# A transformer block on one core: the adaLN front in four channel quarters, head 0 accumulated in six banks

## The chip, the cores and the metric

The program runs on one core of a Trainium2 chip. The core has five engines that run their own instruction streams and meet only through semaphores: TensorE (PE, matmuls), VectorE (DVE), ScalarE (ACT), GpSimd (POOL) and SyncE (SP), which here only issues DMAs. The metric is the device time of one execution in microseconds; lower is better. In the rows, PEld is TensorE's weight load, and SPq is SyncE's queue of DMA issues.

## The reference, cut to what matters

One block (depth 1) on 512 tokens of width 2048, all in float32. Every matrix product that matters is done as three float32r products of a high and a low part.

```
mod = silu(c) @ w_ada + b_ada                    # w_ada (2048, 12288)
sh1, sc1, gt1, sh2, sc2, gt2 = split(mod, 6)     # 2048 channels each
h = rmsnorm(x, g_norm1) * (1 + sc1) + sh1
proj = h @ w_in                                  # mq, mk, mv, mo, 16 gates, aq, ak, av
q, k = silu(conv5(mq)), silu(conv5(mk)) / 16     # 4 heads of 256 channels
gates -> log sigmoid, running sums and maxima per chunk of 128 tokens
m_out = sigmoid(mo) * layernorm(mlstm forward + backward) * g_mlstm_out
a_out = rmsnorm(windowed attention with rope and sinks)
x = x + gt1 * ([m_out, a_out] @ w_out)
h = rmsnorm(x, g_norm2) * (1 + sc2) + sh2
x = x + gt2 * ((silu(h @ w_gate) * (h @ w_up)) @ w_down)
out = rmsnorm(x, g_final)
```

`silu(c) @ w_ada` is a vector times a 100 MB matrix. It isn't done on TensorE: DVE multiplies each 128-row tile of `w_ada` by the matching 128 entries of silu(c), one per partition, and adds it into `acc`; only the sum over the 128 partitions is left to TensorE.

## The kernel before

Activations lie transposed: channels on the partitions, 512 tokens along the free axis, so `h` is 16 tiles of 128x512, `h_hi` and `h_lo`. Projection weights come in slots of 1 MB (2048 columns of `wraw`): ACT makes the high part `whi` (`hi`, L513), POOL (`lo`, L437) or, from the output projection on, DVE makes the low part `wlo`, and TensorE runs 48 matmuls on the slot (`mm3`, L1378 to L1380). There are two buffers of each. The semaphores that tie these together are `w_ld` (loaded), `whi_ok`, `wlo_ok`, and `w_used` (two per slot).

The front, up to head 0, has these parts.

- SP issues 13 loads of constants, then 32 loads of 1 MB of `w_ada` (rows of 4 KB), the four 1 MB blocks of `x`, and the first weight slots, in one order (L301 to L338). `w_ada` goes through a ring of four buffers, and each load waits for DVE's operation four places earlier.
- DVE's loop over those 32 loads (L879 to L897) has the work on `x` put in between by hand: `mean_square` two loads after a block of `x` was asked for, `normalise` three after. ACT squares a block (L499) and copies its transposes out of PSUM (L502), block by block.
- After 16 loads (shift and scale of the first 1024 channels) `ada_turn0` transposes `acc` on TensorE, `ada_take0` sums it, and `h_half` makes eight tiles of `h`: DVE makes `hf` (L857), ACT makes `h_hi` (L521) and DVE makes `h_lo` (L877). Loads 16 to 23 are worked off between them. The second half follows after load 31.
- TensorE does the three first-half slots of q, k and v of head 0 in that time, then, with the second half, the gate slot and the five others (`BODY0`, L243). DVE computes the gate rows (`gate_rows_`, about 60 short operations in a chain on 64 partitions), eight more tiles of `w_ada` (the block's gate vector gt1), and the convolutions of q and k (`conv`, `silu`).

After that a loop over heads 1 to 3, a "tail" and an "end" do eight weight slots a head, the previous head's mLSTM in between, and eight tiles of `w_ada` per body. Every engine's order in them is written out by hand (`body` on each engine). Attention and the output projection (16 slots) take the last 16 tiles of `w_ada`; then comes the feed-forward part.

In this kernel nothing is scheduled by a planner: each engine executes its list in order, and an instruction that waits holds everything behind it on its engine.

Of the kernel before, what the change touches and what calls it, by code (L numbers as in the profile page):

```python
# [41 lines left out]
P = 128  # L42
D = 2048
# [56 lines left out]
def program(nc, x, c, positions, w_ada, b_ada, g1, g2, w_in, b_gates, w_conv, b_conv, gm, sink, ga,  # L100
            w_out, w_gate, w_up, w_down, gf, rope_inv, out):
    ctx = ExitStack()
    with ctx:
# [16 lines left out]
        def region(base, names):  # L120
# [53 lines left out]
        (xnT, xst0, xst1, hf), end0 = region(mix, [  # L174
            ("xnT", [P, KT, S], F32), ("xst0", [P, D], F32), ("xst1", [P, D], F32), ("hf", [P, 2, S], F32)])
        xst = [xst0, xst1]
        (stg, posi, ang, kf, ar2, junk), _ = region(big, [
            ("stg", [P, 3, P], F32), ("posi", [P, S], I32), ("ang", [P, S], F32), ("kf", [P, S], F32),
            ("ar2", [P, S], F32), ("junk", [P, D], F32)])

        (gsb, selI, selZ, li, zz, az, bb, aa, mx, blm, arow), end2 = region(mix, [
            ("gsb", [GATES, S], F32), ("selI", [GATES, 64], F32), ("selZ", [GATES, 64], F32),
            ("li", [64, S], F32), ("zz", [64, S], F32), ("az", [64, S], F32), ("bb", [64, S], F32),
            ("aa", [64, S], F32), ("mx", [64, S], F32), ("blm", [64, 16], F32), ("arow", [64, 10, P], F32)])
# [28 lines left out]
        x_ld = [x_ld, sem("x_ld1")]  # L213
# [4 lines left out]
        ada_acc, ada_sum, modp_ok, mod_ok = map(sem, ["ada_acc", "ada_sum", "modp_ok", "mod_ok"])  # L218
        hhi_ok, hlo_ok = map(sem, ["hhi_ok", "hlo_ok"])
# [27 lines left out]
        NB = 45  # L247
        NC_ = 16

        XLOAD = (0, 3, 8, 11)  # L250
        RING0 = [wraw[0], wraw[1], araw[0], araw[1]]
        RING1 = [xst[0], xst[1], araw[0], araw[1]]

        BODY0 = [(0, 0), (1, 0), (2, 0), None, (0, 1), (1, 1), (2, 1), (3, 0), (3, 1)]
# [9 lines left out]

        def c_bank(u):

            return 4 * ((u + 1) % 2)
# [4 lines left out]
        TURN0 = ((4, 5, 6, 7), (4, 5, 4, 5))  # L272

        def tile_done(h, g, i):

            if isinstance(h, int) and h == 0:
                return 2 * BODY0.index((g, 1)) + 1 + i
            return h * 16 + (4 * g + 5 + i)
# [8 lines left out]
        def _(sp):  # L287
            def rows(v, b=P):
                return v.rearrange("o (a b) -> (o a) b", b=b)

            for dst, src in ((stg[C_G1:C_G1 + 16, 0, :], rows(g1)), (stg[C_G2:C_G2 + 16, 0, :], rows(g2)),
                             (stg[C_GF:C_GF + 16, 0, :], gf.rearrange("(a b) -> a b", b=P)),
                             (stg[C_BC:C_BC + 16, 0, :], rows(b_conv)), (stg[C_GM:C_GM + 8, 0, :], rows(gm)),
                             (stg[C_GA:C_GA + 8, 0, :], rows(ga)), (stg[C_C:C_C + 16, 0, :], rows(c)),
                             (stg[0:96, 1, :], rows(b_ada)),
                             (stg[0:80, 2, :], w_conv.rearrange("o k (a b) -> (o k a) b", b=P)),
                             (sinkb[:], sink[0, :].partition_broadcast(P)),
                             (bgate[:], b_gates.rearrange("o g -> g o")),
                             (posi[:], positions[0, :].partition_broadcast(P)),
                             (invf[:], rope_inv)):  # L300
                sp.dma_start(dst, src).then_inc(const_ld, 16)  # L301

            def w_slot(par, s, col0, kk):
                if isinstance(s, int) and s < 2:
                    sp.wait_ge(ada_acc, 13 + s)
                else:
                    sp.wait_ge(wlo_ok, s - 1)
# [3 lines left out]
            def w_slot0(s):  # L311

                g, kk = BODY0[s]
                w_slot(s % 2, s, slice(g * 1024, g * 1024 + 256), kk)


            for n in range(32):
                ring = RING1 if n >= 16 else RING0
                if n >= 4:
                    sp.wait_ge(ada_acc, n - 3)  # L320
                if n in (16, 17):
                    sp.wait_ge(xT_ps, 4 * (n - 13))
# [1494 lines left out]
```

## Time and profile before

| what | us |
|---|---|
| median of 3 runs (lowest, highest) | 2497.02 (2496.67, 2499.35) |
| span of the profiled execution, first to last instruction | 2496.3 |
| TensorE busy in it | 2325.1 (93%) |
| DVE, ACT, POOL busy | 1211.0, 636.9, 297.4 |
| TensorE idle in the first 248 us | 103 |

The last line is worked out from the stretches 0:140 and 140:248 of the table of windows. The span is within 0.8 us of the median of the runs, so differences in the profiled execution carry over to the time. Most of the span is feed-forward work in which TensorE never stops; the places where it stops are in the first 400 us and around the attention.

### The profile page before, as it was taken

To read this page: it belongs to the slowest core of one execution; us is meant where nothing else is said; L and a number is where in the kernel's file an instruction comes from. 1 tells how busy PE (TensorE), PEld (TensorE's weight loads), DVE (VectorE), ACT (ScalarE), POOL (GpSimd) and SP (SyncE) were. 2 spreads that over 40 slices of the span, in tenths; PEclk is the share of its full clock that TensorE was granted. 3 is DMA by queue.
4 is the path that set the end of the run, shared out by engine and by line. 5 is a ranking of instruction groups with operands and counts; after the bars stand their busy time and mean duration, and the time that the engine had idled before them with its cause. 6 is when DMAs were issued, how large, how long until landed. Compare 5 with 4: busy or idle time off the path is not lost.

```text
span 2496.3 us, 26411 instructions
## 1 busy us (share of the span) xinstructions
PE 2325.1 (93%) x10515; PEld 1924.3 (77%) x10515; DVE 1211.0 (49%) x1395; ACT 636.9 (26%) x720; POOL 297.4 (12%) x100
## 2 busy tenths in 40 slices
PE   1677999999997899899999999999999999999997
PEld 1556878787886788788888888888888888888876
DVE  6878464656567545743333333334343434343334
ACT  2231323223235421332121212121221222222222
POOL 0221333333431111100000000000000000000003
PEclk9888999999998999999999999999999999999998
DMA  8855434253453255133323332332233223323322
GB/s 341 281 176 185 154 133 168 101 185 116 154 206 115 102 184 214 58 102 101 100 86 100 101 97 88 101 101 92 93 101 101 90 95 101 101 86 99 101 94 92
DMA packets 148211, 317.79 MB, mean 127 GB/s; under 512 B 5296, under 2 KB 52672, under 8 KB 138816
## 3 DMA queue, kind: packets, MB, share of 16 engines
q1 hardware_dynamic: 148160, 317.10, 37.1%
q8 instruction: 34, 0.56, 0.1%
q14 instruction: 17, 0.14, 0.0%
HBM read 312.88 MB, written 4.19 MB: 127 GB/s over the span
## 4 chain that ended last, share of the span: by engine, by line
PE 80%; DVE 12%; DMA 3%; issue 3%; ACT 2%; POOL 1%; DVEq 0%; SPq 0%; ACTq 0%; POOLq 0%
PE ps L1378 25%; PE ps L1379 25%; PE ps L1380 25%; DMA araw<-in_w_ada 3%; DVE acc L799 2%; DVE qk L1044 2%; DVE acc L1074 1%; PE ps L1508 1%; DVE qk L1041 1%; PE ps L1521 1%; PE ps L1519 1%; PE ps L1616 1%; DVE h_lo L877 0%; DVE hf L857 0%; DVE sm L1168 0%
## 5 line engine op out<-in xcount | busy, mean ns | idle before, releaser
L1281 DVE TENSOR_TENSOR wlo<-wraw,whi 128x2048 fp32r<-128x2048 f32 x130 | 298.0, 2292 | 609.1 <-ACT whi L732 609.1
L1378 PE MATMUL ps<-f_hi,whi 128*128 128x512 f32 x1408 | 548.8, 390 | 3.7 <-DVE f_lo L1296 2.6
L1379 PE MATMUL ps<-f_lo,whi 128*128 128x512 f32 x1408 | 548.3, 389 | 0.0
L1380 PE MATMUL ps<-f_hi,wlo 128*128 128x512 f32 x1408 | 548.2, 389 | 0.0
L732 ACT ACTIVATE whi<-wraw 128x2048 fp32r<-128x2048 f32 x130 | 248.9, 1915 | 923.7 <-PE ps L1380 923.7
L1378 PEld LDWEIGHTS ps<-f_hi,whi 128*128 128x128 f32 x1408 | 264.7, 188 | 59.5 <-issue 3.2
L1380 PEld LDWEIGHTS ps<-f_hi,wlo 128*128 128x128 f32 x1408 | 264.7, 188 | 55.0
L1379 PEld LDWEIGHTS ps<-f_lo,whi 128*128 128x128 f32 x1408 | 264.8, 188 | 54.7
L1378 PE MATMUL ps<-h_hi,whi 128*128 128x512 f32 x720 | 288.5, 401 | 19.2 <-DVE h_lo L877 15.7
L1379 PE MATMUL ps<-h_lo,whi 128*128 128x512 f32 x720 | 283.8, 394 | 0.0
L1380 PE MATMUL ps<-h_hi,wlo 128*128 128x512 f32 x720 | 283.5, 394 | 0.0
L1378 PE MATMUL ps<-a_hi,whi 128*128 128x512 f32 x704 | 274.8, 390 | 2.2 <-DVE a_lo L1313 2.2
L1380 PE MATMUL ps<-a_hi,wlo 128*128 128x512 f32 x704 | 274.6, 390 | 0.0
L1379 PE MATMUL ps<-a_lo,whi 128*128 128x512 f32 x704 | 274.5, 390 | 0.0
L437 POOL TENSOR_TENSOR wlo<-wraw,whi 128x2048 fp32r<-128x2048 f32 x45 | 211.0, 4688 | 446.2 <-ACT whi L513 446.2
L1320 DVE SCALAR_TENSOR_TENSOR xT<-ps,mod,xT 128x512 f32<-128x512 f32 x176 | 131.7, 750 | 194.3 <-PE ps L1380 194.3
L475 POOL COPY ssum<-sqt 128x512 f32<-128x512 f32 x2 | 4.4, 2216 | 1479.2 <-ACT sqt L709 1479.2
L1378 PEld LDWEIGHTS ps<-h_hi,whi 128*128 128x128 f32 x720 | 137.7, 191 | 51.4 <-POOL wlo L437 9.4
L513 ACT ACTIVATE whi<-wraw 128x2048 fp32r<-128x2048 f32 x45 | 86.0, 1911 | 336.6 <-PE ps L1380 300.9
L1380 PEld LDWEIGHTS ps<-h_hi,wlo 128*128 128x128 f32 x720 | 137.3, 191 | 29.4
L1379 PEld LDWEIGHTS ps<-h_lo,whi 128*128 128x128 f32 x720 | 137.6, 191 | 27.7
L1378 PEld LDWEIGHTS ps<-a_hi,whi 128*128 128x128 f32 x704 | 132.6, 188 | 30.0 <-DVE a_lo L1313 2.6
(237 smaller groups left out, 2352.0 us busy)
## 6 DMA issues: line engine op xcount, KB each, us to landing
araw<-in_w_ada SPq DMA_DIRECT2D x80, 1024.0 KB, 5.8
wraw<-in_w_in SPq DMA_DIRECT2D x45, 1024.0 KB, 5.3
wraw<-in_w_gate SPq DMA_DIRECT2D x44, 1024.0 KB, 5.2
wraw<-in_w_up SPq DMA_DIRECT2D x44, 1024.0 KB, 5.2
wraw<-in_w_down SPq DMA_DIRECT2D x44, 1024.0 KB, 5.0
wraw<-in_w_out SPq DMA_DIRECT2D x16, 1024.0 KB, 7.3
wraw<-in_w_ada SPq DMA_DIRECT2D x8, 1024.0 KB, 10.2
xst<-in_w_ada SPq DMA_DIRECT2D x8, 1024.0 KB, 6.0
```

Of the source, the lines that this page charges most:

```text
L437: pool.tensor_tensor(wlo[par][:], wraw[par][:], whi[par][:].bitcast(F32), ALU.subtract)\
L513: A(whi[par][:], wraw[par][:], ACT.Copy).then_inc(whi_ok, 1)
L732: A(whi[par][:], wraw[par][:], ACT.Copy).then_inc(vhi_ok, 1)
L799: V_.scalar_tensor_tensor(out=acc[:], in0=slot[:], scalar=csil[:, kt:kt + 1], in1=acc[:], op0=ALU.mult, op1=ALU.add).then_inc(ada_acc, 1)
L1041: ch.link(V_.tensor_scalar(qk[:, t, :], convin[:, t, 0:S], cols[:, bass.ds(tile + C_WC, 1)], cols[:, bass.ds(tile + C_BC, 1)], ALU.mult, A ...
L1044: ins = V_.scalar_tensor_tensor(out=qk[:, t, :], in0=convin[:, t, k:k + S], scalar=cols[:, bass.ds(tile + (C_WC + 16 * k), 1)], in1=qk[:, ...
L1074: V_.scalar_tensor_tensor(out=acc[:], in0=araw[par][:], scalar=csil[:, kt:kt + 1], in1=acc[:], op0=ALU.mult, op1=ALU.add).then_inc(ada_acc, 1)
L1281: V_.tensor_tensor(wlo[k % 2][:], wraw[k % 2][:], whi[k % 2][:].bitcast(F32), ALU.subtract)\
L1320: V_.scalar_tensor_tensor(out=xT[:, t, :], in0=ps[bank + i][:], scalar=mod[:, 5, t:t + 1], in1=xT[:, t, :], op0=ALU.mult, op1=ALU.add).the ...
L1378: pe.matmul(o, w_hi, m_hi, start=first, stop=False)
L1379: pe.matmul(o, w_hi, m_lo, start=False, stop=False)
L1380: return pe.matmul(o, w_lo, m_hi, start=False, stop=last)
```

## The change

The front is written anew.

- **Constants.** Their 13 loads are issued from ACT's queue, ahead of ACT's first instruction. SP begins with `x` and `w_ada`.
- **x buffers.** Each of the four blocks of `x` has its own buffer and is loaded at once, before loads 0 to 3 of `w_ada`. On DVE, `mean_square(n)`, the pair of operations on load n, and `normalise(n)` follow each other for n = 0 to 3; the angle work of rope comes behind them. ACT's order is as before: square a block, then copy its four transposes.
- **adaLN.** Shift and scale are made in four quarters of 512 channels. A load is still 1 MB but holds two row tiles of 1024 columns (rows of 2 KB), and DVE runs two operations of 128x1024 on it (`ada_pair`). At a quarter's end TensorE sums over partitions with eight matmuls of one column into bank 5 (`ada_columns`). `hf` is made on ACT, next to `h_hi`.
- **Head 0.** q, k and v come in eight slots of 256 rows by 768 columns (1536 columns of `wraw`). TensorE accumulates six tiles in six banks with the contraction outermost, 36 matmuls a slot. The low parts of these eight slots are made by DVE (`front_lo`). The gate slot and the two slots of o follow, with POOL making their low parts. In number of matmuls this is what it was.
- **Behind it.** On DVE: convolution of q, `gates_in`, convolution of k, `select`, gate rows, `gate_columns`. On TensorE `gate_columns` and `turn_v` stand ahead of head 1's first slot. The eight tiles of gt1 leave head 0's body; all later bodies take the tiles one body earlier in the sequence, and the output projection takes 24 tiles where it took 16, by the tables `LATE_OP` and `LATE_LD`.

The diff, cut to what the prediction speaks of:

```diff
+        LATE_OP = [0, 1, 2, 3, 4, 4, 5, 5, 7, 7, 8, 8, 9, 9, 10, 10, 11, 11, 12, 12, 13, 13, 14, 15]
...
             for n in range(32):
-                ring = RING1 if n >= 16 else RING0
+                quarter, pair = n // 8, n % 8
+                if n < TB:
+                    sp.dma_start(xst[n][:], x[0, n * P:(n + 1) * P, :]).then_inc(x_ld[n], 16)
                 if n >= 4:
-                    sp.wait_ge(ada_acc, n - 3)
...
+                    sp.wait_ge(ada_acc, 2 * (n - 3))
+                for k in range(2):
+                    sp.dma_start(RING[n % 4][:, k * 1024:(k + 1) * 1024].rearrange("p (q c) -> p q c", q=2),
+                                 w_ada[0, pair * 256 + k * P:pair * 256 + (k + 1) * P, 0:2 * D].rearrange(
+                                     "p (q h c) -> p q h c", q=2, h=4)[:, :, quarter, :]).then_inc(ada_ld[n % 4], 16)
+                if pair in (4, 5):
+                    front_slot(2 * quarter + pair - 4)
...
+            pool.wait_ge(wlo_ok, FRONT)
+            for s in range(8, 13):
                 lo(s, s % 2)
-            body(0, False)
...
+            def first():
+
+                act.wait_ge(w_used, 14)
+                hi(8, 0, 9)
+                for t in range(4):
+                    evac(convin[:, t, 2:2 + S], FBANK[t], tile_done(0, t // 2, t % 2))
+                for i in range(2):
+                    evac(vT[:, i, :], 6 + i, tile_done(0, 2, i))
+                act.wait_ge(w_used, 16)
+                hi(9, 1, 9)
+                conv_sigmoids(0, 5)
+                conv_sigmoids(0, 6)
+                act.wait_ge(w_used, 18)
+                hi(10, 0, 10)
+                gates()
+                for s in (11, 12):
+                    act.wait_ge(w_used, 2 * (s - 1))
+                    hi(s, s % 2, s // 2 + 5)
+                exp_minus_m()
+                turned_v(0)
...
+            def h_quarter(quarter):
+
+                part = slice(4 * quarter, 4 * quarter + 4)
+                dve.wait_ge(ada_sum0, quarter + 1)
                 for q in range(2):
-                    last = V_.tensor_tensor(mod[:, q, part], modp[:, q, part],
+                    last = V_.tensor_tensor(mod[:, q, part], ps[5][:, 8 * quarter + 4 * q:8 * quarter + 4 * q + 4],
                                             cols[:, C_BA + 16 * q + part.start:C_BA + 16 * q + part.stop], ALU.add)
...
+            for n in range(32):
+                quarter, pair = n // 8, n % 8
+                if n < TB:
+                    mean_square(n)
+                ada_pair(n)
+                if n < TB:
+                    normalise(n)
+                if n == 3:
                     trig()
-                if n == 3:
+                if n == 4:
                     trig_round(2048.0)
-                if n == 4:
+                if n == 5:
                     trig_round(1.0)
                     trig_end()
+                if pair >= 6:
+                    front_lo(2 * quarter + pair - 6)
+                if pair == 7:
+                    h_quarter(quarter)
...
+            conv_pair(0, 0)
+            gates_in()
+            conv_pair(0, 2)
+            select(0)
+            gate_rows_()
+            gate_columns()
```

How the lists of instructions stand. First DVE's from its first addition into `acc` on, before; `tiny` is `mean_square`, the operation on `xst0` is `normalise`, `ang` and `kf` belong to rope:

```order
L796 TENSOR_SCALAR acc_74<-wraw0_66,csil_55 128x2048 [waits ada_ld0,silu_ok]
L799 SCALAR_TENSOR_TENSOR acc_74<-wraw1_67,csil_55,acc_74 128x2048 [waits ada_acc,ada_ld1]
L799 SCALAR_TENSOR_TENSOR acc_74<-araw0_72,csil_55,acc_74 128x2048 [waits ada_acc,ada_ld2]
L820 TENSOR_SCALAR tiny_63<-tiny_63 128x1 [waits ssq_ok]
L830 CAST ang_100<-posi_99 128x512 [waits const_ld]
```

The same place of DVE's list now:

```order
L823 TENSOR_SCALAR tiny_63<-tiny_63 128x1 [waits ssq_ok,silu_ok]
L865 TENSOR_SCALAR acc_74<-fr0_95,csil_55 128x1024 [waits ada_ld0]
L868 SCALAR_TENSOR_TENSOR acc_74<-fr0_95,csil_55,acc_74 128x1024 [waits ada_acc]
L828 TENSOR_SCALAR xst0_98<-xst0_98,tiny_63 128x2048 [waits rsx_ok]
L823 TENSOR_SCALAR tiny_63<-tiny_63 128x1 [waits ssq_ok]
L868 SCALAR_TENSOR_TENSOR acc_74<-fr1_96,csil_55,acc_74 128x1024 [waits ada_acc,ada_ld1]
L868 SCALAR_TENSOR_TENSOR acc_74<-fr1_96,csil_55,acc_74 128x1024 [waits ada_acc]
L828 TENSOR_SCALAR xst1_99<-xst1_99,tiny_63 128x2048 [waits rsx_ok]
L823 TENSOR_SCALAR tiny_63<-tiny_63 128x1 [waits ssq_ok]
```

Three operations on `w_ada` stood ahead of the first wait for ACT's squares (`ssq_ok`) and many between it and the second; now each of the first four loads has that wait in front of it.

The second place is ACT's list from the last `h_hi` of head 0 on, now; `whi` is the high part of a weight slot, `convin` and `vT` are the copies of q, k and v, `Pt` the sigmoids of the convolution, `az` the gates:

```order
L522 ACTIVATE h_hi_75<-xnT_94,mod_54 128x512
L509 ACTIVATE whi0_68<-wraw0_66 128x2048 [waits w_ld0,w_used]
L539 ACTIVATE convin_85<-ps0 128x512 [waits w_used]
L539 ACTIVATE vT_87<-ps7 128x512 [waits w_used]
L509 ACTIVATE whi1_69<-wraw1_67 128x2048 [waits w_ld1,w_used]
L580 ACTIVATE Pt_89<-qk_84 128x512 [waits conv_pre] x4
L509 ACTIVATE whi0_68<-wraw0_66 128x2048 [waits w_ld0,w_used]
L528 ACTIVATE az_113<-az_113 64x512 [waits gate_rows]
```

The high part of the last slot of o stands behind all four sigmoids. Before, ACT's list had the gates and three high parts ahead of the sigmoids:

```order
L513 ACTIVATE whi_69<-wraw_67 128x2048 [waits w_ld1,w_used]
L532 ACT_TABLE_LOAD
L532 ACTIVATE az<-az 64x512 [waits gate_rows]
L534 ACT_TABLE_LOAD
L534 ACTIVATE az<-az 64x512 [waits gate_exp]
L543 ACTIVATE convin<-ps 128x512 [waits w_used] x2
L513 ACTIVATE whi_68<-wraw_66 128x2048 [waits w_ld0,w_used]
```

So the gates moved from ahead of the convolutions to behind them, on ACT as on DVE.

## Rows read from the trace of the kernel before

**Rows 1.** The page: busy time of TensorE, and DVE's low part of a 2048-column slot.

```profile
PE 2325.1 (93%) x10515; PEld 1924.3 (77%) x10515; DVE 1211.0 (49%) x1395; ACT 636.9 (26%) x720; POOL 297.4 (12%) x100
...
L1281 DVE TENSOR_TENSOR wlo<-wraw,whi 128x2048 fp32r<-128x2048 f32 x130 | 298.0, 2292 | 609.1 <-ACT whi L732 609.1
```

**Rows 2.** Windows: stretch and length, busy us by engine (count), granted clock, DMA share, GB/s.

```profile
0.00:140.00 140.00, 53.80 (x227) 42.73 (x227) 111.87 (x82) 35.05 (x42) 22.63 (x20) 0.86 0.87 312
140.00:248.00 108.00, 90.85 (x375) 72.96 (x376) 85.71 (x122) 28.53 (x30) 27.79 (x6) 0.85 0.46 159
```

**Rows 3.** Timeline, one block of x: start us, us, engine line op, out<-in, [idle before].

```profile
54.59 1.28 DVE L825 TENSOR_SCALAR xst<-xst,tiny 128x2048 f32<-128x2048 f32 x1
55.93 3.77 PE L1396 MATMUL ps<-ident,xst 128*128 128x128 f32 x16 [9.70 <-DVE xst L825]
60.23 1.90 ACT L499 ACTIVATE junk<-xst 128x2048 f32<-128x2048 f32 x1
62.26 0.15 DVE L820 TENSOR_SCALAR tiny<-tiny 128x1 f32<-128x1 f32 x1
```

**Rows 4.** Timeline, the start and the first half's shift and scale.

```profile
6.00 0.43 SPq L301 DMA_DIRECT2D invf<-rope_constants  x1
11.13 0.18 DVE L789 TENSOR_TENSOR csil<-cols,tiny 128x16 f32<-128x16 f32 x1 [0.28 <-ACT tiny L493]
33.96 2.14 DVE L838 SCALAR_TENSOR_TENSOR ang<-kf,ang 128x512 f32<-128x512 f32 x3
73.51 0.17 DVE L850 SCALAR_TENSOR_TENSOR mod<-mod,cols 128x8 f32<-128x8 f32 x1
```

**Rows 5.** Timeline, operations on w_ada and h around the second half.

```profile
115.20 4.81 DVE L799 SCALAR_TENSOR_TENSOR acc<-xst,csil,acc 128x2048 f32<-128x2048 f32 x2
140.32 3.93 PE L1422 MATMUL ps<-ident,acc 128*128 128x128 f32 x16 [17.25 <-DVE acc L799]
147.74 5.76 ACT L521 ACTIVATE h_hi<-xnT,mod 128x512 fp32r<-128x512 f32 x8 [4.94 <-DVE mod L850]
148.91 0.69 DVE L877 TENSOR_TENSOR h_lo<-hf,h_hi 128x512 fp32r<-128x512 f32 x1
```

**Rows 6.** Timeline, POOL beside DVE.

```profile
185.07 4.75 POOL L437 TENSOR_TENSOR wlo<-wraw,whi 128x2048 fp32r<-128x2048 f32 x1 [4.61 <-ACT whi L513]
185.40 4.51 DVE L959 COPY arow<-aa 32x128 f32<-32x128 f32 x1
192.61 0.22 DVE L959 COPY arow<-aa 32x128 f32<-32x128 f32 x1
```

**Rows 7.** Timeline, the gate rows, their columns, the convolutions of q, head 1's start.

```profile
166.53 0.68 DVE L919 COPY li<-ps 32x512 f32<-32x512 f32 x1 [6.28 <-PE ps L1483]
200.80 0.14 DVE L964 COPY arow<-arow 1x1 f32<-1x1 f32 x1
205.29 1.90 PE L1489 MATMUL ps<-ident,az 64*128 64x36 f32 x8
227.86 0.54 DVE L1041 TENSOR_SCALAR qk<-convin,cols 128x512 f32<-128x512 f32 x1
235.08 1.47 DVE L1054 SCALAR_TENSOR_TENSOR qk<-qk,Pt 128x512 f32<-128x512 f32 x2
242.35 0.79 PE L1378 MATMUL ps<-h_hi,whi 128*128 128x512 f32 x1 [2.57 <-POOL wlo L437]
```

**Rows 8.** Windows: DMA with 4 KB rows of w_ada, then with 2 KB rows of w_gate.

```profile
16.00:44.00 28.00, 5.19 (x23) 4.45 (x24) 24.98 (x24) 6.36 (x9) 1.37 (x2) 1.00 1.01 390
1246.00:1248.00 2.00, 2.00 (x11) 1.65 (x10) 1.30 (x3) 0.63 (x1) 0.00 (x0) 1.00 1.02 399
```

**Rows 9.** Timeline, TensorE: the 12th and 48th matmul of head 1's first slot; 16 transposes.

```profile
247.20 0.48 PE L1380 MATMUL ps<-h_hi,wlo 128*128 128x512 f32 x1
255.51 0.39 PE L1380 MATMUL ps<-h_hi,wlo 128*128 128x512 f32 x1
...
896.79 1.91 PE L1668 MATMUL ps<-ident,xs 128*128 128x128 f32 x16
```

More of the change, by code:

```diff
@@ L600, in body @@
                         exps(m, j, m * 4)
-                    if j == 0 and kind == "first":
-                        gates()
-                    if j == 5 and kind == "first":
-                        for i in range(2):
-                            evac(vT[:, i, :], 6 + i, tile_done(0, 2, i))
-                        exp_minus_m()
                     if j == 2:
@@ L632, in body @@
                     if j == 7:
[L633 to L636 removed]
+                        turned_v(h)
                     if kind == "end" and j in (1, 3):
@@ L886, in _ @@
-            for n in [*range(16), *range(20, 32)]:
-                ada0(n)
-                if n - 2 in XLOAD:
-                    mean_square(XLOAD.index(n - 2))
-                if n - 3 in XLOAD:
-                    normalise(XLOAD.index(n - 3))
-                if n == 2:
+            for n in range(32):
+                quarter, pair = n // 8, n % 8
+                if n < TB:
[4 more added lines that the diff above has]
+                if n == 3:
@@ L1090, in body @@
                 for j in range(steps):
-                    if kind == "first" and j == 5:
-                        gate_columns()
                     for i in (range(2 * j, 2 * j + 2) if kind == "end" else
@@ L1455, in _, with ada_columns @@
-            slot0(1)
-            slot0(2)
-            ada_turn0(1)
-            pe.wait_ge(wlo_ok, 4)
-            pe.wait_ge(modp_ok, 16)
+            def ada_columns(quarter):
+                pe.wait_ge(ada_acc, 16 * (quarter + 1))
+                for j in range(8):
+                    c = quarter % 2 * 1024 + j * P
+                    last = pe.matmul(ps[5][:, 8 * quarter + j:8 * quarter + j + 1], acc[:, c:c + P], ones[:, 0:1],
+                                     start=True, stop=True)
+                last.then_inc(ada_sum0, 1)
@@ new lines, in _ @@
+            for s in range(FRONT):
+                if s % 2 == 0:
+                    ada_columns(s // 2)
+                pe.wait_ge(wlo_ok, s + 1)
+                for k in range(2):
+                    kt = 2 * s + k
+                    pe.wait_ge(hlo_ok, kt + 1)
+                    for t in range(6):
+                        c = k * FCOLS + t * P
+                        last = mm3(ps[FBANK[t]][:], whi[s % 2][:, c:c + P], wlo[s % 2][:, c:c + P], h_hi[:, kt, :],
+                                   h_lo[:, kt, :], kt == 0, kt == KT - 1)
+                        if k == 1 and t in (2, 5):
+                            last.then_inc(w_used, 1)
@@ L1545, in body @@
                 for j in range(steps):
-                    if kind != "first":
-                        slot(h, j)
-                    elif j >= 3:
-                        slot0(1 + j)
-                    if kind == "first" and j == 5:
-                        gate_columns()
+                    slot(h, j)
                     if mixing and j == 0:
```

409 lines of the change are left out of this document (182 added, 227 removed).

## Prediction

> **What bounds the kernel now.** I read the busy shares first: TensorE works 93% of the span [rows 1], 171 of 2496 us idle. The table of windows then says where: 86 us of the idle time lie in the first 140 us and 17 in the next 108 [rows 2]. So all that this change can win or lose lies before about 250 us, apart from what it moves into the output projection. In that stretch TensorE is not the bound: it waits for `h`, and `h` waits for DVE. DVE is busy 112 of 140 and 86 of 108 us [rows 2]; DMA runs at 312 GB/s on average in the first and at 390 where it is pressed [rows 8]. The event to follow is the first matmul of head 1, at 242.35 [rows 7]: from there on both kernels have the same list up to the attention, and TensorE rarely stops. Shift and scale of the first half are ready at 73.5 [rows 4]; the gate rows run from 166.5 to 200.9, then come eight tiles of gt1, then the convolutions from 227.9 [rows 7].
>
> I walk the new lists along these durations, with C for the moment when silu(c) is ready and T0 to T3 for the four moments when a quarter's shift and scale are.
>
> **Start.** Before, the last constant was issued at 6.0 to 6.4 and silu(c) was there at 11.3 [rows 4]. ACT now issues the same 13 loads, but beside up to 8.4 MB that SP has asked for. Bounds: 11.3, as before, and 23 or so, if they come behind all of it at 390 GB/s. I take C = 12.7, near the row, as they stand on a queue of their own.
>
> **The x blocks.** This is the step I trust most. DVE's `mean_square(n)` waits for ACT's square of block n, and that stands in ACT's list behind the four copies of block n-1, which need TensorE's transposes, which need `normalise(n-1)` on DVE. From the end of a `normalise` (55.87) to the next `mean_square` (62.26) is 6.4 us [rows 3]. Before, DVE did one to three tiles of w_ada in that time. Now it waits, since the pair on load n stands behind `mean_square(n)`. One block costs 6.4, plus 0.15, the pair, and 1.28 for `normalise` [rows 3]. The pair: 2048 columns take 2.35 us and follow each other at 2.46 (two in 4.81), 512 columns take 0.69 [rows 5]; by a straight line 1024 take 1.24, with the gap 1.33, so a pair is 2.65. That is 10.6 us a block. The first `mean_square` is at C + 2.1 (square of 1.9, and 0.2), so the fourth `normalise` ends at C + 2.1 + 0.15 + 2.0 + 1.3 + 3 x 10.6 = C + 37.4. DVE idles 6.4 us three times, 19 us in all, and a ring of four loads stops DMA as well.
>
> **The first quarter.** Behind it: 0.95 for the angle's start, three pairs (7.95), two rounds of about 3.1 (2.14 for three of their five operations [rows 4]) and 0.45, to C + 53; the small ones here and below are of 0.2 to 0.75 us each. The low part of slot 0 waits for ACT, which has rope's sines (2.1 us) and a 1536-column high part (1.45) behind that chain: C + 53.9, done at C + 55.7 (1.75 for 1536 columns, between 0.69 for 512 and 2.29 for 2048 [rows 1, 5]). The last pair ends at C + 58.3. `ada_columns` are 16 weight loads and passes on a TensorE that has stood for 10 us; 16 transposes on such an engine took 3.93 [rows 5]. With 0.6 for three small operations T0 = C + 62.8 = 75.5. Before, half the channels were ready at 73.5; now a quarter.
>
> **A quarter.** From shift and scale on, ACT makes `hf` and `h_hi` of four tiles, eight operations in 5.8 us, and the last `h_lo` follows 0.75 later [rows 5]: 6.5. Then 16 operations on w_ada, 20.6; one low part, 1.75 (the second hides under `ada_columns`); 4.0 for these, 0.6 for the rest: 33.5. DMA must bring 8.4 + 1.6 MB in that time, 25 us at 399 GB/s, which 2 KB rows reach [rows 8], or 32 us at the 312 of the first 140 us [rows 2]; in the latter case the late loads of a burst cost up to 2.5. I take 0.5: 34.0 a quarter, and T3 = 177.5. TensorE's 72 matmuls fit in between. Head 1's first slot shows their price: it began after a pause with the first 12 at the lower clock (1.2 GHz), 4.85 us for 11 of them, and from there to the 48th they came 0.23 us apart, at 2.4 GHz [rows 7, 9]. So 72 x 0.228 = 16.4, and 12 x 0.2 = 2.4 for such a start: 18.8.
>
> The Trainium skill (DMA: Bandwidth & Descriptors, Specifications) gives 512 B as the least transfer for line rate. By that rule rows of 2 KB cost nothing, the 0.5 goes and the time is 1.5 us lower; the 399 GB/s above agree, while a stretch that mixes in the 1 KB rows of w_in fell to 312.
>
> **From T3 to head 1.** TensorE starts slot 6 at T3 + 2.2 and ends slot 7 18.8 later; q's two tiles end 9 matmuls before that, and two copies bring DVE's convolution to T3 + 20.2. From here one chain runs on DVE: two pairs of convolutions with their products, 7.2 + 1.4 each [rows 7], `gates_in` 0.75, `select` 0.35, the gate rows. These took 34.4 (166.5 to 200.9) [rows 7], of which three operations stood still for 4.3 beside POOL's low parts: a copy of 0.22 us took 4.51 while POOL was at it from 185.07 [rows 6]. Without them 21.6. Now POOL makes four low parts in this chain (slots 9 to 12), as ACT makes each high part behind work that the chain itself releases: 4 x 4.3 = 17.2. Sum 57.1, so the gate rows end at T3 + 77.3. TensorE has finished the second slot of o at T3 + 62 and stands. Then `gate_columns` 6.2 (to 207.19) [rows 7], a copy of 0.7, `turn_v` 2.0 (eight of the 16 transposes in 3.93 [rows 5]), 0.2 between: T3 + 86.4 = 263.9 against 242.35, **21.5 us later**. Before, the gate rows were computed beside five slots of matmuls, and the 27 us of gt1 behind them are what the change takes away here; it gets less than it pays for the three quarters in series and the gates put last.
>
> The Trainium skill (SBUF — State Buffer, SBUF: two separate sides) says that GpSimd excludes only a VectorE operation with two SBUF inputs or in a two-port mode, so the four copies out of PSUM at the head of the gate rows could run beside slot 10's low part. The sum would be about 2 us lower. The rows of before, a copy of SBUF among them, agree that what is locked out waits for the whole of it.
>
> **Late part.** Eight tiles move to the output projection. TensorE gets 16 transposes more, 1.9 us [rows 9], and I count them in full, as it has no gaps there. DVE gets 19 us more in 14 slots of 10.9; its work per four slots (low parts 9.2, w_ada 19, copies and sums 8) stays under 43.6, so I cost it at nothing. If that cover fails, at the reads of one accumulator where TensorE waits for `acc`, it costs up to 5.
>
> **Sum.** 2496.3 + 21.5 + 1.9 = 2519.7; with the 0.7 by which the median of the runs lies above the profiled span, 2520 us. Its own range: C from -1.4 to +10, quarters -1.5 to +6, fewer collisions with POOL -8.6, the clock -2 to +4, late part 0 to +5. They won't fall on one side together: 2508 to 2538.
>
> **Rivals.**
> - Faster: DVE's total decides, not its order. Before head 1 the change takes eight tiles (8 x 2.35 = 19) and `hf` (16 operations, about 9) from DVE and adds eight low parts (14) and the gaps of 32 more operations (5); POOL makes five low parts fewer there, worth 4.3 each where they collide and nothing where DVE idles, of which I count 6. That is 15 us less. If DVE idled no more than the 50 us it now does in 248, head 1 would start so much earlier: 2496.3 - 15 + 1.9 + 0.7 = 2484. For it: DVE is 80% busy there [rows 2]. Against it: the 19 us at the x blocks and 4 x 10 at the quarters' ends are idle time written into the lists. It decides if DVE's waits before head 1 stay under 55 us.
> - Constants late: they come behind the bulk loads, C near 23: 2530. For it, SP's first 12 issues are all large; against it, they fill another queue.
> - No change: the new front costs what gt1 gave, about 20 us, because the gate rows overlap better than I think and POOL collides once or twice rather than four times. It needs 12 us from there and 10 from the quarters: 2498.
>
> **Chances.** Forecast 0.75, constants late 0.10, faster 0.10, no change 0.05. A measurement of this kernel tells a change from none at about 0.2%, 5 us. Faster by more than that 0.09, within it 0.05, slower 0.86. The range for 8 in 10 runs from 2500 to 2540; it leaves out the faster case and the far ends.
>
> **What will show it.** Right: four squares of x on ACT some 10.6 us apart, with DVE waiting 6 us before each of the last three; shift and scale at about 75, 110, 144 and 178; gate rows ending near 255; TensorE idle from about 240 to 255; head 1's first matmul near 264; TensorE full in the output projection. Wrong: head 1 before 245, a quarter under 31 us, or DVE not waiting for the squares; then it is the faster case. The first DVE operation on w_ada after 20 us would be the late constants.

## The result, and the profile after

| | median us | lowest to highest | runs |
|---|---|---|---|
| before | 2496.85 | 2496.43 to 2499.35 | 4 |
| changed | 2523.97 | 2522.54 to 2526.04 | 4 |

The changed kernel is slower: ratio 1.0106, 95% interval 1.0091 to 1.0121, or 27.1 us. The forecast was slower, 2520 us, range 2500 to 2540. The profiled execution has a span of 2524.3, 28.0 more than before, and took 2526.04 in all, 2 us above its median. One of the six executions of a kernel further down (narrow lows on GpSimd) took 4805 us; its ratio leaves that one out, and why it was so long is not known.

Busy times on the page, then the table of windows of the first two stretches (columns as in [rows 2]), both of the changed kernel:

```profile
PE 2340.9 (93%) x10547; PEld 1940.2 (77%) x10547; DVE 1196.8 (47%) x1409; ACT 655.8 (26%) x743; POOL 273.1 (11%) x94
```

```profile
0.00:140.00 140.00, 60.23 (x243) 49.35 (x243) 80.22 (x85) 42.05 (x52) 7.52 (x16) 0.93 0.70 247
140.00:248.00 108.00, 81.49 (x324) 65.77 (x324) 76.94 (x96) 31.31 (x36) 18.88 (x4) 0.81 0.47 159
```

DVE is busy 80 of the first 140 us, where it was busy 112 [rows 2]. DMA fell from 312 to 247 GB/s with it, since the ring of loads waits for DVE. The stretch up to head 1's first matmul, before and then changed, says how much of this is less work and how much is waiting:

```profile
0.00:242.35 242.35, 139.00 (x587) 111.24 (x588) 192.18 (x195) 62.95 (x71) 50.42 (x26) 0.86 0.69 244
0.00:269.84 269.84, 149.64 (x603) 122.78 (x604) 170.01 (x212) 76.88 (x91) 30.89 (x21) 0.85 0.58 200
```

Before head 1 DVE is busy 22 us less (what it stands beside POOL counts as busy in both), and it is idle 99.8 us where it was 50.2. Head 1's first matmul shows what it comes to: 269.84 against 242.35 [rows 7], 27.5 us later. The last matmul of that slot is at 282.62 against 255.51 [rows 9], and the whole is 28.0 longer. The loss is all in front of head 1.

The timeline of the changed kernel (start us, us, engine line op, out<-in, [idle before]), first the start:

```profile
7.12 0.45 ACTq L486 DMA_DIRECT2D invf<-rope_constants  x1
16.93 0.71 PE L1401 MATMUL ps<-ident,stg 96*128 96x96 f32 x3 [16.93 <-DMA invf<-rope_constants]
18.40 0.17 DVE L801 TENSOR_TENSOR csil<-cols,tiny 128x16 f32<-128x16 f32 x1 [0.28 <-ACT tiny L489]
28.13 1.90 ACT L495 ACTIVATE junk<-xst 128x2048 f32<-128x2048 f32 x1
30.15 0.15 DVE L823 TENSOR_SCALAR tiny<-tiny 128x1 f32<-128x1 f32 x1 [6.45 <-ACT junk L495]
32.75 1.28 DVE L828 TENSOR_SCALAR xst<-xst,tiny 128x2048 f32<-128x2048 f32 x1
40.42 0.15 DVE L823 TENSOR_SCALAR tiny<-tiny 128x1 f32<-128x1 f32 x1 [6.38 <-ACT junk L495]
78.77 0.16 DVE L853 SCALAR_TENSOR_TENSOR mod<-mod,cols 128x4 f32<-128x4 f32 x1
```

The last constant was issued at 7.6 and TensorE began on the constants at 16.93, 9.4 us later (before, 3.3 us after the last issue); silu(c) was ready at 18.6 instead of 11.3 [rows 4]. Then the waits for the squares: 6.45 and 6.38 us (a third of 6.38 at 50.69), one block every 10.3 us. Before, a block cost DVE no wait of this kind [rows 3].

One quarter, the second (`fr` and `araw` are the ring of loads):

```profile
103.32 2.61 DVE L868 SCALAR_TENSOR_TENSOR acc<-araw,csil,acc 128x1024 f32<-128x1024 f32 x2 [2.28 <-DMA araw<-in_w_ada]
113.78 0.23 DVE L882 TENSOR_TENSOR mod<-ps,cols 128x4 f32<-128x4 f32 x2 [2.00 <-PE ps L1433]
114.04 0.16 DVE L853 SCALAR_TENSOR_TENSOR mod<-mod,cols 128x4 f32<-128x4 f32 x1
115.86 0.69 DVE L890 TENSOR_TENSOR h_lo<-hf,h_hi 128x512 fp32r<-128x512 f32 x1 [1.65 <-ACT h_hi L522]
117.27 0.69 DVE L890 TENSOR_TENSOR h_lo<-hf,h_hi 128x512 fp32r<-128x512 f32 x1 [0.72 <-ACT h_hi L522]
```

Three kinds of wait: for a late load, for TensorE's column sums, and for ACT before each `h_lo`. And POOL beside DVE between the last quarter and head 1, then TensorE's way to head 1:

```profile
210.53 7.34 DVE L1054 SCALAR_TENSOR_TENSOR qk<-convin,cols,qk 128x512 f32<-128x512 f32 x4
210.65 5.10 POOL L419 TENSOR_TENSOR wlo<-wraw,whi 128x2048 fp32r<-128x2048 f32 x1 [4.95 <-ACT whi L509]
229.68 4.53 POOL L419 TENSOR_TENSOR wlo<-wraw,whi 128x2048 fp32r<-128x2048 f32 x1 [13.94 <-ACT whi L509]
230.85 0.68 DVE L930 COPY zz<-ps 32x512 f32<-32x512 f32 x1
231.56 3.18 DVE L931 SCALAR_TENSOR_TENSOR az<-zz 64x512 f32<-64x512 f32 x1
238.18 5.99 DVE L944 TENSOR_TENSOR_SCAN bb<-ones,zz 64x128 f32<-64x128 f32 x4
250.29 4.43 DVE L970 COPY arow<-aa 32x128 f32<-32x128 f32 x1
261.07 0.14 DVE L974 COPY arow<-arow 1x1 f32<-1x1 f32 x1
261.27 4.48 PE L1479 MATMUL ps<-ident,arow 64*128 64x36 f32 x20 [13.15 <-DVE arow L974]
269.84 0.78 PE L1393 MATMUL ps<-h_hi,whi 128*128 128x512 f32 x1
282.94 1.98 PE L1487 MATMUL ps<-mnat,sel 64*128 64x512 f32 x4
```

Four DVE groups stand still beside POOL; the gate rows end at 261.2 instead of 200.9 [rows 7]; TensorE stands 13.15 us for them.

### The profile page after: what moved, and what is told of

Its sections match the earlier page's. It is cut to its first block, busy times and chain, and to the rows that moved or that the text cites. A ratio compares the mean times of both kernels' runs of the same rounds, so it can differ in the third digit from the quotient of the medians.

```text
span 2524.3 us, 26554 instructions
## 1 busy us (share of the span) xinstructions
PE 2340.9 (93%) x10547; PEld 1940.2 (77%) x10547; DVE 1196.8 (47%) x1409; ACT 655.8 (26%) x743; POOL 273.1 (11%) x94
## 3 DMA queue, kind: packets, MB, share of 16 engines
q1 hardware_dynamic: 156160, 316.69, 36.7%
## 4 chain that ended last, share of the span: by engine, by line
PE 80%; DVE 11%; issue 3%; ACT 3%; DMA 2%; POOL 0%; ACTq 0%; DVEq 0%; SPq 0%; POOLq 0%
PE ps L1393 24%; PE ps L1394 24%; PE ps L1395 24%; DVE acc L868 2%; DVE qk L1054 2%; DMA araw<-in_w_ada 1%; PE ps L1498 1%; DVE acc L1084 1%; DVE qk L1051 1%; PE ps L1511 1%; PE ps L1509 1%; PE ps L1433 1%; PE ps L1610 1%; PE ps L1421 1%; PE ps L1411 0%
## 5 line engine op out<-in xcount | busy, mean ns | idle before, releaser
L744 ACT ACTIVATE whi<-wraw 128x2048 fp32r<-128x2048 f32 x130 | 248.9, 1915 | 923.6 <-PE ps L1395 923.6
L419 POOL TENSOR_TENSOR wlo<-wraw,whi 128x2048 fp32r<-128x2048 f32 x39 | 183.9, 4715 | 510.8 <-ACT whi L509 510.8
L509 ACT ACTIVATE whi<-wraw 128x2048 fp32r<-128x2048 f32 (+1 forms) x47 | 86.3, 1839 | 293.9 <-PE ps L1395 248.6
```

The costliest lines, as they stand in the source:

```text
L419: pool.tensor_tensor(wlo[par][:], wraw[par][:], whi[par][:].bitcast(F32), ALU.subtract)\
L509: A(whi[par][:, 0:width], wraw[par][:, 0:width], ACT.Copy).then_inc(whi_ok, 1)
L744: A(whi[par][:], wraw[par][:], ACT.Copy).then_inc(vhi_ok, 1)
```

## The experiments

All eleven start from the changed kernel (2524.0), some with several edits at once; each ratio is against the kernel before, run on the same chip in the same session.

| kernel | median us | ratio to before, 95% |
|---|---|---|
| squares first | 2504.9 | 1.0028 (1.0017 to 1.0039) |
| constants first | 2518.3 | 1.0085 (1.0072 to 1.0099) |
| slot under the gate rows | 2514.9 | 1.0072 (1.0059 to 1.0086) |
| next pair first | 2510.6 | 1.0053 (1.0039 to 1.0067) |
| these four together | 2482.1 | 0.9938 (0.9925 to 0.9951) |
| ... without the constants' edit | 2482.9 | 0.9943 (0.9928 to 0.9957) |
| four, and lows after a pair | 2474.4 | 0.9906 (0.9892 to 0.9921) |
| ... and lows of slots 8 to 12 on VectorE | 2463.7 | 0.9861 (0.9846 to 0.9877) |
| narrow lows on GpSimd | 2512.6 | 1.0059 (1.0046 to 1.0071) |
| high part of slot 10 early | 2526.6 | 1.0117 (1.0103 to 1.0132) |
| late transposes twice | 2525.2 | 1.0109 (1.0092 to 1.0126) |

### 1. Squares first

```diff
@@ ACT
                 A(junk[:], xst[tb][:], ACT.Square, accum_out=ssq[:, tb:tb + 1]).then_inc(ssq_ok, 1)
+            for tb in range(TB):
                 for q in range(4):
```

> ScalarE does the four squares of x one after another, each as soon as its block of x is there, and only then the sixteen copies of transposed x out of PSUM. Nothing else changes. Theory A (the x chain is serial because the next square stands behind four copies on ScalarE, and VectorE waits for it): the three VectorE waits of 6.4 us in the first 60 us go, the first quarter's shift and scale are ready 17 to 19 us earlier (about 61 instead of 78.9), and the whole is 2505 to 2507 against 2524 for the changed kernel. Rival (the ring of w_ada loads is the real limit of that stretch, which ran at 204 to 333 GB/s): VectorE's waits turn into waits for DMA, and less than half comes through, 2515 or more.

19.1 us faster. The timeline of this kernel's DVE, its first waits gone:

```profile
22.47 1.28 DVE L829 TENSOR_SCALAR xst<-xst,tiny 128x2048 f32<-128x2048 f32 x1
23.67 0.14 DVE L824 TENSOR_SCALAR tiny<-tiny 128x1 f32<-128x1 f32 x1
26.25 1.28 DVE L829 TENSOR_SCALAR xst<-xst,tiny 128x2048 f32<-128x2048 f32 x1
```

A block takes 3.8 us instead of 10.3, and the first quarter is ready at 59.4, 19.5 earlier. The three waits of the prediction's x blocks (19 us) are shown as their full price, and the loads didn't take their place.

### 2. Constants first

```diff
@@ SP, ahead of the first block of x (removed from ACT)
+                sp.dma_start(dst, src).then_inc(const_ld, 16)
```

> The thirteen small constant loads are issued by SyncE again, in front of the first block of x, instead of by ScalarE beside it. Theory B (they came at 16.9 us only because their small packets shared the DMA engines with 1 MB transfers): silu(c) is ready near 12 instead of 18.6 us, VectorE starts its first pair 6 to 7 us earlier, and since nothing hides that start, the whole is 2517 to 2518 against 2524. Rival: the first block of x and the first pairs come later by the thirteen issues, VectorE waits for those instead, and the time stays within 2 us of 2524.

5.6 us faster. In this kernel's timeline silu(c) is 7.6 us earlier, but the first blocks come later: DVE waits 3.05 us for ACT's square where it waited 1.80, and then for the first load of `w_ada`:

```profile
10.83 0.17 DVE L802 TENSOR_TENSOR csil<-cols,tiny 128x16 f32<-128x16 f32 x1 [0.28 <-ACT tiny L490]
14.87 0.75 DVE L866 TENSOR_SCALAR acc<-fr,csil 128x1024 f32<-128x1024 f32 x1 [0.65 <-DMA fr<-in_w_ada]
```

The first operation on `w_ada` starts 5.6 us sooner (20.44 in the changed kernel), which is the gain. The edit changes two things at once, the queue and the place ahead of the bulk; constants on ACT's queue with the bulk held back were not tried.

### 3. A slot under the gate rows

```diff
@@ PE
                     slot(h, j)
+                    if kind == "peeled" and j == 0:
+                        gate_columns()
+                        pe.wait_ge(gcol_sb, 1)
+                        turn_v(0, False)
...
-            gate_columns()
-            pe.wait_ge(gcol_sb, 1)
-            turn_v(0, False)
-            with pe.Fori(1, HEADS) as h:
+            body(1, "peeled")
+            with pe.Fori(2, HEADS) as h:
```

> On TensorE alone the body of head 1 is written out before the loop, and its first slot of 48 matmuls goes ahead of the fourteen gate column matmuls and head 0's turned v, which wait for the gate rows of VectorE. Theory C (TensorE stands idle for about 13 us before the gate columns, because they are in front of head 1 in its program): that slot fills the idle time, head 1's second slot starts 11 to 13 us earlier, and the whole is 2511 to 2513 against 2524. Rival: the slot's weights or the banks are not free then, or the clock falls for the filled time, and 6 us or less comes through, 2518 or more.

9.1 us, under what the theory gave (11 to 13) and over the rival. TensorE's timeline in this kernel:

```profile
259.80 4.46 PE L1479 MATMUL ps<-ident,arow 64*128 64x36 f32 x20 [3.54 <-DVE arow L974]
268.64 3.78 PE L1487 MATMUL ps<-mnat,sel 64*128 64x512 f32 x4
272.35 3.78 PE L1498 MATMUL ps<-qk 128*128 128x128 f32 x16
```

The idle time shrank from 13.15 to 3.54, and the spread begins 14.3 us earlier than at 282.94. But the spread and the 16 matmuls of scores now come right behind the pause and take 3.78 us each, against 1.98 and 2.05. The granted clock from 268.6 to 277.0 is 0.51 in this kernel, so 1.2 GHz, and 1.00 over the same work in the changed one (282.9 to 287.0). The rival's mechanism took 3.5 us back. Another 1.5 of the 14.3 us belong to the two profiled executions and not to the edit: the gate columns start that much earlier here, on a DVE list that is the same.

### 4. The next pair first

```diff
@@ DVE
                 ada_pair(n)
+                if pair == 0 and quarter:
+                    h_quarter(quarter - 1)
...
-                if pair == 7:
-                    h_quarter(quarter)
+                if n == 31:
+                    h_quarter(3)
```

> VectorE does the first pair of the next quarter before it takes the summed shift and scale of the quarter just done; so TensorE's column sums run beside that pair, and the next slot of the ring comes free one step sooner. Theory E1 (each of the first three quarters costs VectorE a wait of 2.0 us for TensorE's column sums and about 2.3 us for DMA behind it): both go in three quarters, 6 to 12 us in all, 2512 to 2518 against 2524. Rival E2 (the ring's transfers at 308 to 375 GB/s are the limit of a quarter): what VectorE no longer waits for TensorE it waits for DMA, and the time stays at 2522 to 2524.

13.3 us, more than the 12 of the theory's upper end. DVE in this kernel's timeline:

```profile
107.34 1.28 DVE L868 SCALAR_TENSOR_TENSOR acc<-fr,csil,acc 128x1024 f32<-128x1024 f32 x1
108.64 0.23 DVE L882 TENSOR_TENSOR mod<-ps,cols 128x4 f32<-128x4 f32 x2
108.90 0.16 DVE L853 SCALAR_TENSOR_TENSOR mod<-mod,cols 128x4 f32<-128x4 f32 x1
```

No wait before the sums, and a quarter is 31 us instead of 35.9 (the next two end at 140.25 and 171.17). Of DMA waits one of 0.54 is left from 9. So the loads were not too slow on the average of a quarter; they were late because the ring had stopped while DVE stood, and then had to catch up (from 95 to 103 us of the changed kernel DMA is at a share of 1.05 with 375 GB/s, into the wait that ends at 103.32). The prediction had counted them as bytes over a rate.

### 5. Four edits together

> The four edits of the first call together: squares first on ScalarE, constants first from SyncE, head 1's first slot under the gate rows, VectorE's next pair before the sums of a quarter. If they are four separate pieces of one serial path, their gains add: 19.1 + 5.6 + 9.1 + 13.3 = 47.1 us below the changed kernel's 2524, so about 2477, and 20 us under the kernel before. Rival (the transfers of the first quarter, some 14 to 16 MB in the 45 us that are left, become the limit): VectorE waits for DMA in the first 60 us, 5 to 12 us do not come through, 2482 to 2489.

2482.1, 41.9 us of the 47.1, at the edge of the rival. Timeline and windows of this kernel:

```profile
22.02 2.61 DVE L870 SCALAR_TENSOR_TENSOR acc<-fr,csil,acc 128x1024 f32<-128x1024 f32 x2 [1.19 <-DMA fr<-in_w_ada]
```

```profile
10.00:35.00 25.00, 4.84 (x22) 3.92 (x21) 14.50 (x18) 10.39 (x13) 2.22 (x4) 1.00 1.02 389
```

From 10 to 35 us DMA is at its full share, 389 GB/s. DVE waits for four loads, 3.2 us in all, and 2.8 us more for the squares of the later three blocks. A block of x with its pair is 2 MB, 5.4 us at that rate, where DVE alone needed 3.8. Whether that is the missing 5 us is asked by the next one.

### 6. Without the constants' edit

> The kernel with four edits, but with the constants on ScalarE's queue again as in the changed kernel, so three edits. It tests where 5.2 us of the four edits' summed gain (47.1 expected, 41.9 measured) went. Theory (with the squares first the loads of x and w_ada set the first 35 us, at 396 to 398 GB/s and 2 MB a block of x with its pair, so it hardly matters when silu(c) is ready): the time is only 0 to 2 us above the 2482.1 of the four edits. Rival (the constants' edit keeps its own 5.6 us and another of the four lost): 2487 to 2489.

2482.9, within 0.8 us of the four edits: the constants' edit gives nothing once the squares come first. The first quarter is ready at 59.0 in this kernel's timeline and at 60.6 with all four, so silu(c) at 18.2 or at 11.1 makes no difference. With the waits for loads in experiment 5, this shows the loads as the cause of the missing gain.

### 7. Lows after a pair

```diff
@@ DVE, in the loop over n, h_quarter ending before its four h_lo
+                if pair == 1 and quarter:
+                    h_lows(quarter - 1)
```

> On top of the four edits, in the first three quarters VectorE does one more pair of w_ada between the shift and scale of a quarter and the four low parts of h, so that it no longer waits for ScalarE before each of them (1.65 us, then three times 0.72 us, a quarter). Theory (VectorE's own program is the path): 3.8 us in each of three quarters, 11 us below the kernel with four edits. Rival (the loads are the limit as soon as a quarter is under about 30 us, 10 MB at 320 to 340 GB/s): VectorE waits for DMA instead, and 0 to 5 us comes through.

7.7 us below the four edits, between the two. Windows and timeline of this kernel:

```profile
60.00:120.00 60.00, 43.79 (x179) 35.80 (x180) 55.11 (x54) 21.17 (x27) 0.00 (x0) 0.78 1.00 352
```

```profile
87.40 0.16 DVE L855 SCALAR_TENSOR_TENSOR mod<-mod,cols 128x4 f32<-128x4 f32 x1
115.51 0.16 DVE L855 SCALAR_TENSOR_TENSOR mod<-mod,cols 128x4 f32<-128x4 f32 x1
```

A quarter is 28.1 us. DMA is at a share of 1.00 with 352 GB/s, and still no DVE operation of this stretch waits for it; what did not come through is 0.3 to 0.7 us before the last two or three `h_lo`, since ACT's pace is one in 1.4 us. DVE is 92% busy: these quarters are at both limits at once.

### 8. Narrow lows on GpSimd

```diff
@@ POOL
-                lo(s, s % 2)
+                pool.wait_ge(whi_ok, s + 1)
+                pool.tensor_tensor(wlo[s % 2][:, 0:64], wraw[s % 2][:, 0:64],
+                                   whi[s % 2][:, 0:64].bitcast(F32), ALU.subtract).then_inc(wlo_ok, 1)
```

> The changed kernel, but GpSimd makes only 64 of the 2048 columns of the low parts for slots 8 to 12, so those five slots are multiplied with old low parts in the rest (this part of the computation is left out); two short GpSimd instructions at the start fill the unwritten columns. Theory (four VectorE instructions of the gate rows and the convolution each stood still while GpSimd was in a 4.7 us subtraction, 15.1 us in all): VectorE's path from the last quarter to the end of the gate rows is 12 to 15 us shorter and the whole 2509 to 2512. Rival (VectorE's path there is hidden behind TensorE, ScalarE and the slots, or the waits come back elsewhere): 4 us or less, 2520 or more.

11.4 us by the median of all six executions, 12.2 by that of the five without the one of 4805 us, so at the small end of the theory. The kernel leaves out most of five low parts. Three of the places on DVE's timeline in this kernel:

```profile
210.52 3.12 DVE L1059 SCALAR_TENSOR_TENSOR qk<-convin,cols,qk 128x512 f32<-128x512 f32 x4
218.06 0.74 DVE L928 TENSOR_SCALAR gsb<-ps,bgate 16x512 f32<-16x512 f32 x1 [3.03 <-PE ps L1400]
234.56 1.76 DVE L949 TENSOR_TENSOR_SCAN bb<-ones,zz 64x128 f32<-64x128 f32 x4
```

Four collisions cost 4.2, 2.5, 4.2 and 4.2, 15.2 us together (each a group's length with POOL beside it, less its length here). Of these 3.0 are now a wait for the gate slot's matmuls instead, and 12.0 are left between the convolution and the gate columns. Where one wait hides behind another, taking the first away does not win its whole length.

### 9. The high part of slot 10 early

```diff
@@ ACT
                 conv_sigmoids(0, 5)
-                conv_sigmoids(0, 6)
                 act.wait_ge(w_used, 18)
                 hi(10, 0, 10)
+                conv_sigmoids(0, 6)
```

> The changed kernel, but ScalarE makes the high part of slot 10 (o's second half) between the first and the second pair of convolution sigmoids instead of behind both, so TensorE's slots before the gate columns can end earlier. Theory (VectorE's gate rows, not the slots, release the gate columns; TensorE stands idle 13.2 us before them): no change within 2 us, 2522 to 2526. Rival (TensorE's slots are the path there): 4 to 9 us, 2515 to 2520.

2526.6 against 2524.0, not faster, and 0.6 above the theory's range. TensorE's and DVE's timelines in this kernel:

```profile
261.39 4.48 PE L1479 MATMUL ps<-ident,arow 64*128 64x36 f32 x20 [21.11 <-DVE arow L974]
```

```profile
218.80 7.49 DVE L1054 SCALAR_TENSOR_TENSOR qk<-convin,cols,qk 128x512 f32<-128x512 f32 x4
244.40 4.80 DVE L946 TENSOR_TENSOR aa<-li,bb 64x512 f32<-64x512 f32 x1
```

TensorE ended its slots 8 us earlier and stood 8 us longer, 21.11 instead of 13.15. The gate rows end where they did, although this execution had its last shift and scale 1.6 us earlier: POOL's subtraction came earlier and met a convolution instead of `az`, and two in a row met the scan and the subtraction behind it. The slots are not the path here.

### 10. Lows on VectorE

```diff
@@ DVE
+            whole_lo(8)
-            conv_pair(0, 0)
+            conv_pair(0, 0, 9)
             gates_in()
-            conv_pair(0, 2)
+            conv_pair(0, 2, 10)
             select(0)
             gate_rows_()
+            whole_lo(12)
             gate_columns()
```

(`conv_pair` makes the low part named ahead of its silus, and slot 11's is in `gate_rows_` behind the scans; ACT as in experiment 9.)

> On top of the kernel with four edits and the lows after a pair (2474.4), the low parts of slots 8 to 12 are made by VectorE (2.35 us each) instead of GpSimd (4.7 us each): slot 8's in VectorE's 12 us wait for the convolution's input, 9's and 10's before the silus, 11's behind the first scans, 12's behind the last gate row; and ScalarE makes slot 10's high part between the two pairs of convolution sigmoids. Theory (VectorE is shut out while GpSimd subtracts, 15 us in all, against some 7 us that it now spends itself where nothing hid it): the gate rows end 8 us earlier, TensorE's slots just keep up, and the whole is 2464 to 2469. Rival (VectorE's own subtractions cost what the shutting out did, or TensorE's slots become the path): 2472 or more.

2463.7, 10.7 us below the kernel of experiment 7, just past the good edge of what was expected, and the fastest of all: 33.9 us, 1.4%, under the kernel before. Timelines of DVE and TensorE in this kernel:

```profile
194.76 1.77 DVE L952 TENSOR_TENSOR_SCAN bb<-ones,zz 64x128 f32<-64x128 f32 x4
196.56 2.29 DVE L955 TENSOR_TENSOR wlo<-wraw,whi 128x2048 fp32r<-128x2048 f32 x1
```

```profile
211.63 2.90 PE L1498 MATMUL ps<-ident,arow 64*128 64x36 f32 x20 [0.71 <-DVE arow L984]
```

The scans take 1.77 again, the low part 2.29, and TensorE's pause before the gate columns is 0.71 us: DVE's path and TensorE's slots now end together. What the earlier high part of slot 10 does in this kernel was not tried by itself.

### 11. The late transposes twice

```diff
@@ PE, ada_turn
+                    for again in range(2 if isinstance(hidx, int) and hidx == 14 else 1):
                         for i in range(4):
```

> The changed kernel, but the sixteen transposes that the change adds in the output projection (the accumulator of w_ada's fourth late part) are done twice over, into the same banks. The prediction put these sixteen at 1.9 us on the path; between the two traces the output projection grew by only 0.3 us, while a wait of 1.27 us for VectorE that stood in the kernel before is gone. Theory (TensorE is the path there: sixteen transposes cost 1.9 us, and the wait that went paid for most of the first sixteen): TensorE needs 1.9 us more for that stretch, 2525 to 2527. Rival (transposes there fall into time that TensorE waits anyway): 0, 2524.

1.25 us above the changed kernel, less than a comparison of medians can tell, so the trace has to say it. TensorE's timeline, first of the changed kernel, then of this one:

```profile
983.88 1.91 PE L1421 MATMUL ps<-ident,acc 128*128 128x128 f32 x16
1018.29 1.91 PE L1662 MATMUL ps<-ident,xs 128*128 128x128 f32 x16
```

```profile
982.68 3.65 PE L1422 MATMUL ps<-ident,acc 128*128 128x128 f32 x32
1018.84 1.91 PE L1663 MATMUL ps<-ident,xs 128*128 128x128 f32 x16
```

From the one to the other is 34.41 us and 36.16: sixteen transposes cost 1.75 us on the path. That supports the first half of the theory. The second half rests on one row of the kernel before, its 1.27 us wait for DVE's sum of `acc` behind the first of its two groups of such transposes (920.32; the other, at 1015.97, closes the output projection):

```profile
923.49 0.50 PE L1378 MATMUL ps<-o_hi,whi 128*128 128x512 f32 x1 [1.27 <-DVE modp L806]
```

The changed kernel has three such groups and no such wait. That this is why the output projection grew by so little was not tried by itself.

## Why the prediction was right, step by step

| step | predicted | measured | difference |
|---|---|---|---|
| silu(c), C | 12.7 | 18.6 | +5.9 |
| C to T0 | 62.8 | 60.4 | -2.4 |
| three quarters | 102.0 | 107.7 (35.3, 36.7, 35.7) | +5.7 |
| T3 to the end of the gate rows | 77.3 | 74.6 | -2.7 |
| from there to head 1 | 9.1 | 8.6 | -0.5 |
| head 1's first matmul | 263.9 | 269.8 | +5.9 |
| what is added after it | 1.9 | 0.5 | -1.4 |

Sign and mechanism held: DVE's written order set the time, in series with ACT and TensorE. The span is 4.6 us above the sum (2524.3 against 2519.7), because two terms were too small, by 11.6 us, and the others too large, by 7.0. That these two met so nearly is luck; the terms themselves are off by up to 6 us.

- **Start.** A mis-sized term: C was taken as 12.7 and measured 18.6. I put it near the row of before because the constants stood on a queue of their own. A queue of their own did not keep them clear of the bulk: the DMA engines were 92% busy in the first 20 us of the changed kernel, at 333 GB/s. That the sharing of these engines made the constants late, and not ACT's queue as such, is argued and not shown (experiment 2). Experiment 2 gave the price, 5.6 us. The rival "constants late" had the right mechanism, and about half of its size.
- **The x blocks.** Right: waits of 6.45, 6.38 and 6.38 for 6.4 each, 10.3 for 10.6 a block; experiment 1 took all 19.
- **The first quarter.** Right within 2.4 us, of which 1.4 are the blocks.
- **A quarter.** The step on DMA failed. DVE waited 2.28, 3.83 and 2.82 us for loads in the three quarters where I took 0.5, two of them above even the 2.5 that I had named as the bound. The rest of a quarter came out at 32.9 to 33.0 for 33.5. The term was worked out from a quarter's bytes over a rate. Experiment 4 shows that the average rate was not the cause: with DVE's wait for the column sums gone the waits for loads went too, but for one of 0.54 us, although the bytes had to come in less time.
- **Row length.** The Trainium skill's rule on 512 B (DMA: Bandwidth & Descriptors, Specifications) was weighed there as a reason to drop the 0.5. The waits that came were longer and went with DVE's stop, and no run here changes the row length alone, so none shows whether the rule holds for them. The 312 GB/s that I set beside it came at a share of 0.87 [rows 2], so it is no rate of full engines. At a full share, the kernel of experiment 7 shows 352 GB/s with rows of 2 KB and 1 KB (share 1.00), and that of experiment 5 389 with rows of 8 KB and 2 KB (1.02). With the 399 of w_gate's 2 KB rows [rows 8], 2 KB rows are near the best rate seen; whether the 1 KB rows alone account for the difference was not tried.
- **From T3 to head 1.** Four collisions as forecast, 15.2 us for 17.2. Copies out of PSUM did run beside POOL (230.85, 0.68 us, inside POOL's 229.68 to 234.21), and `az` behind them, which reads SBUF twice, stood until POOL had ended (2.5 us where I took 4.3). That is the two-input rule of the Trainium skill (SBUF — State Buffer, SBUF: two separate sides), which the sum had left out: the trace agrees, with 1.8 of the 2.7 us. Two inputs in SBUF are not what every one of the four had: the copy of `aa` (250.29, 4.43 us) has one, and stood as long as the others. What I had not seen is that a collision's length is not its worth: without the collisions, 3.0 us come back as a wait for the gate slot (experiment 8).
- **TensorE stands before the gate columns.** Right: 13.15 us, where 15 was forecast. Experiment 9 makes it longer at no gain, experiment 3 fills it.
- **Late part.** The 16 transposes do cost 1.75 (experiment 11), near the 1.9. The step I missed is what came back, 1.4 us; a wait of 1.27 us in the kernel before, gone in the new order, has that size, but that it is the cause was not tried.
- **The rivals.** "DVE's total decides" is out: up to head 1 DVE was busy 22 us less, and head 1 came 27.5 us later; it waited 99.8 us, where this rival needed under 55. The new front wins only when such waits are taken out: with the squares first, the column sums covered and TensorE's idle time filled by 15 us (experiment 5), and with the lows later and the collisions gone too by 33.9 us (experiment 10), more than the 13 that this rival gave it. "No change" fell with the four collisions.

How much of those 33.9 us the old front could have had by the same edits was not tried; before, the gate rows did not hold TensorE up [rows 7], so experiments 3 and 10 point at little to win there. Nor was the gates' new place behind the convolutions tried against the old one by itself, so how much of the 27 us is due to that one move stays open.

## What to carry to other kernels

When work is taken off the busiest engine of a stretch and the stretch gets longer, read its list for places where it waits for an answer to what it has just issued: each round trip (here to ACT's square, to TensorE's sums, to ACT's `h_hi`) wants one piece of its other work between question and answer, and moving a line or a few gave 19, 13 and 8 us. A late load behind such a stop is a symptom of a stopped ring; take the stop away before counting bytes. And edits that are worth something alone need not add: the constants' 5.6 us vanished once the loads were the limit.

## What was not expected of the hardware

- Thirteen loads of constants (0.41 MB together), issued on ACT's queue between 0.7 and 7.6 us beside 0.5 and 1 MB transfers of SP, were complete 9.4 us after the last was issued; on SP's queue ahead of the same transfers, silu(c) was there 7.6 us sooner.
- Beside POOL's 4.5 to 5.1 us subtraction DVE's reads of PSUM went on at 0.68 us each, and the next one with two SBUF inputs stood for the rest of it. Of a group of four instructions one pays, 4.2 us. Subtractions of 64 columns cost DVE nothing that shows.
- After 3.5 us without work and 36 small matmuls, 20 matmuls of the next steps took 7.6 us instead of 4.0, at a granted clock of 0.51 (experiment 3), so a pause costs more than its length when short work follows it.
